# A fused transformer program on one core: token sums moved from GpSimd to VectorE, and a new order of VectorE's and ScalarE's work inside the feed-forward units

## The reference

```python
def swiglu(h, w1, w3, w2):
    return (jax.nn.silu(h @ w1) * (h @ w3)) @ w2      # w1, w3: 1024 x 2816, w2: 2816 x 1024

h = modulate(rms_norm(x), sh2, sc2)                   # layers 1 and 2
x = x + g2[:, None, :] * swiglu(h, ffn_w1[layer], ffn_w3[layer], ffn_w2[layer])
...
x = x + 0.5 * swiglu_2(rmsnorm(x, ffn1_norm[l]), ffn1_w_gu[l], ffn1_w_down[l])   # before and after the last mixer
```

## Time and profile before

| what | value |
|---|---|
| median of 3 executions | 2495.84 us (2491.64 to 2504.05) |
| the profiled execution: its own time | 2495.73 us |
| the profiled execution: span | 2493.9 us |
| mean granted clock of PE | 0.977 of full speed |
| PE busy | 2379.2 us, 95% |
| DVE busy | 1653.4 us, 66% |
| ACT busy | 999.2 us, 40% |
| POOL busy | 225.8 us, 9% |
| mean DMA rate | 130 GB/s |

### The profile page before, as it was taken

One profiled execution on the slowest core, in us unless ns is written; L12 is line 12 of the kernel. 1 busy time (PEld: TensorE's weight loads), 2 busy tenths in 40 slices (PEclk: granted clock), 3 DMA queues, 4 the chain that ended last, 5 costly groups with the idle time before them and its releaser, 6 DMA issues. The chain is left out here.

```text
span 2493.9 us, 35153 instructions
## 1 busy us (share of the span) xinstructions
PE 2379.2 (95%) x14848; PEld 2112.3 (85%) x14848; DVE 1653.4 (66%) x1985; ACT 999.2 (40%) x1369; POOL 225.8 (9%) x189
## 2 busy tenths in 40 slices
PE   7979999899999989999989999999999999999998
PEld 6658899888899869998869997879889877899986
DVE  6687689757755656884277885456678545688844
ACT  3453343323444443442243442244456544443322
POOL 0210301000013020000040000000000002300000
PEclk9998999999999999999989999999999999999999
DMA  8124577655233126663326653222212212466421
GB/s 347 65 84 186 164 225 205 194 208 196 70 125 104 57 70 175 179 155 119 102 86 166 188 137 123 89 95 85 85 46 74 85 68 85 123 180 170 131 100 68
DMA packets 71727, 325.04 MB, mean 130 GB/s; under 512 B 7850, under 2 KB 9130, under 8 KB 49810
## 3 DMA queue, kind: packets, MB, share of 16 engines
q1 hardware_dynamic: 51984, 238.75, 27.8%
q0 software_dynamic: 16208, 78.13, 13.1%
q10 hardware_dynamic: 3378, 5.91, 0.9%
HBM read 320.52 MB, written 2.24 MB: 129 GB/s over the span
## 5 line engine op out<-in xcount | busy, mean ns | idle before, releaser
L240 PE MATMUL bank<-h_hi,w_hi 128*128 128x256 f32 (+1 forms) x1512 | 512.9, 339 | 30.0 <-DVE w_lo L908 17.9
L241 PE MATMUL bank<-h_lo,w_hi 128*128 128x256 f32 (+1 forms) x1512 | 502.6, 332 | 0.0
L242 PE MATMUL bank<-h_hi,w_lo 128*128 128x256 f32 (+1 forms) x1512 | 502.5, 332 | 0.0
L227 DVE TENSOR_TENSOR w_lo<-raw,w_hi 128x2048 fp32r<-128x2048 f32 x120 | 279.4, 2329 | 145.2 <-ACT w_hi L223 145.2
L240 PEld LDWEIGHTS bank<-h_hi,w_hi 128*128 128x128 f32 x1512 | 291.9, 193 | 67.3 <-DVE w_lo L908 20.9
L242 PE MATMUL bank<-t_hi_tile,w_lo 128*128 128x256 f32 x1152 | 326.0, 283 | 0.0
L240 PE MATMUL bank<-t_hi_tile,w_hi 128*128 128x256 f32 x1152 | 326.0, 283 | 0.0
L241 PE MATMUL bank<-t_lo_tile,w_hi 128*128 128x256 f32 x1152 | 326.0, 283 | 0.0
L242 PEld LDWEIGHTS bank<-h_hi,w_lo 128*128 128x128 f32 x1512 | 291.5, 193 | 27.2
L241 PEld LDWEIGHTS bank<-h_lo,w_hi 128*128 128x128 f32 x1512 | 291.9, 193 | 26.0 <-issue 1.4
L240 PE MATMUL bank<-g_hi,w_hi 128*128 128x512 f32 x704 | 276.9, 393 | 17.6 <-DVE w_lo L227 9.0
(11 more groups left out here) (363 smaller groups left out, 4284.8 us busy)
## 6 DMA issues: line engine op xcount, KB each, us to landing
raw<-stream SPq DMA_DIRECT2D x120, 1024.0 KB, 4.9
raw<-stream SPq DMA_DIRECT2D x72, 512.0 KB, 4.5
work<-stream SPq DMA_DIRECT2D x72, 512.0 KB, 7.1
work<-stream POOLq DMA_DIRECT2D x72, 512.0 KB, 5.8
work<-stream POOLq DMA_DIRECT2D x19, 1024.0 KB, 7.2
raw<-stream SPq DMA_DIRECT2D x72, 256.0 KB, 5.9
h_plain<-stream POOLq DMA_DIRECT2D x16, 1024.0 KB, 5.3
work<-stream SPq DMA_DIRECT2D x13, 1024.0 KB, 12.3
```

What stands on the lines that cost most here:

```text
L227: nc.vector.tensor_tensor(w_lo[:, slot(m), :], raw[:, slot(m), :], w_hi[:, slot(m), :], ALU.subtract).then_inc(lo_split, 1)
L240: nc.tensor.matmul(out, stationary[0], moving[0], start=first, stop=False)
L241: nc.tensor.matmul(out, stationary[0], moving[1], start=False, stop=False)
L242: return nc.tensor.matmul(out, stationary[1], moving[0], start=False, stop=last)
```

## The change

It edits only the feed-forward stages, in six places.

1. The five token sums run on DVE (`hidden_sums`), behind the first unit's split in ffn0 and ffn1 and behind the second's in ffn2 and ffn3; there ACT writes the scaled tokens (`hidden_scaled`). POOL is left with DMAs alone. `hidden_high` and `hidden_low` follow accordingly, the low part one unit later than before.
2. In each fast unit `make_further` stands behind `mixes_low`, and `whole_low` directly behind `add_last`, ahead of `gate_chunk`. `make_further(0)` moves in the same way.
3. SP's loads of unit r wait for `make_further(r - 2)` ("s4") as well. The mixes of units 0 and 1 get a place of their own, and their load waits for the norm's last low part (`h_ready`) instead of `hidden_low`.
4. The conditioning additions stand at r = 1, 3, 5, 7, 9, 11, 14, the first ahead of the loop, and `write_mod` ahead of `add_last(16)`.
5. At the border, ACT makes `pair_high(0)` and the high part of `md` ahead of `keep_first(17)`.
6. PE's first down unit runs both halves over the four early banks before it turns to the last unit's four banks, and there waits for `add_last(17)` instead of `gate_chunk(17)`.

```diff
             def load(self, sp, m):
                 sp.wait_ge(lo_split, m - 1)
+                if r >= 2:
+                    sp.wait_ge(part_lo, self.part_low("s4", r - 2))
...
-                sp.wait_ge(part_lo, self.hidden_lows(2) if r < 2 else self.part_low("mixes", r - 2))
-                sp.dma_start(self.mixes[s], src[:, q:3 * q]).then_inc(landed[s], 16)
+                if r < 2:
+                    sp.wait_ge(h_ready, KC * self.norm.n + KC)
+                else:
+                    sp.wait_ge(part_lo, self.hidden_lows(3) if r < 4 else self.part_low("mixes", r - 2))
+                sp.dma_start(self.mixes(r), src[:, q:3 * q]).then_inc(landed[s], 16)
...
+            def hidden_scaled(self, act):
+                for k in range(KC):
+                    ins = nc.scalar.activation(self.norm.t[:, k, :], x[:, k, :], ACT.Copy, scale=self.norm.scale(k))
+                ins.then_inc(part_hi, 1)
+
+            def hidden_sums(self, dve, st):
+                if self.norm.deferred:
+                    dve.wait_ge(part_hi, self.hidden_highs(1))
...
+                    ins = nc.vector.tensor_tensor(out, one, two, ALU.subtract)
+                    if i < 4:
+                        st.link(ins)
+                ins.then_inc(part_lo, 1)
...
             def scalar(self, act, st):
                     if j < 2:
                         split_next_hi(act, m)
-                    if j == 0:
+                    if j == 0 and self.norm.deferred:
+                        self.hidden_scaled(act)
+                    if j == self.norm.deferred:
                         self.hidden_high(act)
...
                     if r + 1 < FAST:
                         self.whole_high(act, r + 1)
+                    else:
+                        self.pair_high(act, 0)
+                        act.wait_ge(products, self.product_done(4, r))
+                        split_hi(act, self.md)
                     self.keep_first(act, r)
                     if r + 1 < FAST:
                         self.mixes_high(act, r + 1)
-                self.pair_high(act, 0)
-                act.wait_ge(products, self.product_done(4, FAST - 1))
-                split_hi(act, self.md)
...
             def vector(self, dve, st):
                     if j < 2:
                         split_next_lo(dve, self.m0 + j)
-                    if j == 0:
+                    if j == self.norm.deferred:
+                        self.hidden_sums(dve, st)
+                    if j == 1 + self.norm.deferred:
                         self.hidden_low(dve)
                     if j == self.CONV - 2:
-                        self.make_further(dve, 0)
                         self.whole_low(dve, 0)
+                        if self.ada:
+                            dve.wait_ge(part_lo, self.hidden_lows(3))
+                            conditioning.add_unit(dve, 3 * KC)
                 self.mixes_low(dve, 0)
-                if self.ada:
-                    conditioning.add_unit(dve, 3 * KC)
+                self.make_further(dve, 0)
                 for r in range(FAST):
                     self.further_low(dve, r)
+                    if self.ada and r == FAST - 1:
+                        conditioning.write_mod(dve, st, 3)
                     if r:
                         self.add_last(dve, r - 1)
                     if r + 1 < FAST:
-                        self.make_further(dve, r + 1)
+                        self.whole_low(dve, r + 1)
                     if r:
                         self.gate_chunk(dve, r - 1)
                     if r + 1 < FAST:
-                        self.whole_low(dve, r + 1)
                         self.mixes_low(dve, r + 1)
+                        self.make_further(dve, r + 1)
...
                     self.add_first(dve, r)
-                    if self.ada and r and r % 2 == 0 and r < 16:
-                        conditioning.add_unit(dve, 3 * KC + r // 2)
+                    if self.ada and r in (1, 3, 5, 7, 9, 11, 14):
+                        conditioning.add_unit(dve, 3 * KC + 1 + (1, 3, 5, 7, 9, 11, 14).index(r))
...
                     if first:
-                        order = [(k, o) for k in range(2) for o in others + early + after]
+                        order = [(k, o) for k in range(2) for o in others + early] + [(k, o) for k in range(2) for o in after]
...
                         if first and k == 0 and o == after[0]:
-                            pe.wait_ge(gated, self.j0 + FB)
+                            pe.wait_ge(halves_added, self.added(4, late))
```

More of the change, by code:

```diff
@@ L783, in block, with mixes @@
                 return self.weights({"a12": 0, "a11": 1, "a22": 2, "s3": 4, "s1": 5, "s2": 6, "s4": 7}[n], 1)
+            def mixes(self, r):
+                return area((21504 if r < 2 else 4096) + UNIT // 2 * (r % 2), UNIT // 2)
             def mixes_in(self, r):
@@ L789, in part_done @@
             def part_done(self, name, r):
-                return self.hidden_highs(2) + 3 * r + {"mixes": 1, "further": 2, "first": 3}[name]
+                return self.hidden_highs(2 + self.norm.deferred) + 3 * r + {"mixes": 1, "further": 2, "first": 3}[name]
             def part_low(self, name, r):
-                return self.hidden_lows(2) + 4 * r + {"s2": 1, "s4": 2, "mixes": 3, "further": 4}[name]
+                return self.hidden_lows(3) + 4 * r + {"mixes": 1, "s2": 2, "s4": 3, "further": 4}[name]
             def product_done(self, n, r):
@@ L816, in add_parts @@
                 pool.wait_ge(landed[s], landings(self.fast(r)))
-                pool.dma_start(self.mixes[s], stream[place_of(self.fast(r)), :, 2 * q:], accum_op=ALU.add).then_inc(
+                pool.dma_start(self.mixes(r), stream[place_of(self.fast(r)), :, 2 * q:], accum_op=ALU.add).then_inc(
                     mixed_in[s], 16)
             def gpsimd(self, pool):
-                t = self.norm.t
-                if self.norm.deferred:
[L824 to L830, removed]
+                if self.ada:
+                    pool.wait_ge(ada_used, 24)
+                    pool.wait_ge(h_ready, KC * self.norm.n + KC)
+                    for n in range(24, 26):
+                        load_ada(pool, n)
+                for r in range(FAST):
+                    self.add_parts(pool, r)
+                    if self.ada and r in (2, 4, 6, 8, 10, 14):
+                        n = 26 + (2, 4, 6, 8, 10, 14).index(r)
+                        pool.wait_ge(ada_used, n if n == 31 else n - 1)
+                        load_ada(pool, n)
+            def hidden_scaled(self, act):
[3 more added lines that the diff above has]
+            def hidden_sums(self, dve, st):
+                if self.norm.deferred:
+                    dve.wait_ge(part_hi, self.hidden_highs(1))
+                v = self.norm.t.rearrange("p (a z) n -> p a z n", z=2)
                 n = self.HALF
@@ L917, in mixes_high @@
                     act.wait_ge(unit_used, self.fast(0))
-                nc.scalar.activation(self.weights(4, 2)[0], self.mixes[s], ACT.Copy).then_inc(part_hi, 1)
+                nc.scalar.activation(self.weights(4, 2)[0], self.mixes(r), ACT.Copy).then_inc(part_hi, 1)
             def mixes_low(self, dve, r):
@@ L1221, in tensor @@
                         self.norm.spread_row(pe)
[L1222 removed]
+                pe.wait_ge(part_lo, self.hidden_lows(3))
                 for r in range(FAST):
```

34 lines of the change are left out of this document (8 added, 26 removed).

## The result

| | before | after |
|---|---|---|
| median | 2494.67 us (2490.76 to 2504.05, 7 executions) | 2517.3 us (2510.84 to 2518.1, 7 executions) |
| ratio, 95% interval | | 1.0085 [1.0068, 1.0102] |
| span of the profiled execution | 2493.9 us | 2515.3 us |

The change makes the kernel slower by 22.6 us, 0.9%. The forecast was +7.9 us, in a range that ends at 2520.

What follows compares the result with a forecast made beforehand. PE, busy 95%, was taken to bound the kernel, with DVE's rounds exceeding its pace after the change. Fast units and border +27.9, down order -1.5, prologue -18.5 gave +7.9 us: 2504 us, 8 in 10 range 2488 to 2520.

Steps and rivals of the forecast that it cites:

- rival A: The forecast itself: fast-unit rounds of 10.40 and 11.12 us, own range 2494 to 2515 us; chance 0.64.
- B: Fast units: the transfer loop takes over at 11.4 us per unit, +24 us, 2528 us; chance 0.12.
- D: Prologue: sums on DVE only shift the wait, 10 us of the 18.5 are missing, 2514 us; chance 0.12.
- The round: Fast units: DVE's time per unit becomes 10.40 us, 11.12 where the norm is deferred, against PE's 10.08.
- the 1.93 us of the gate and the pair: Fast units: gate_chunk (0.60) and make_further's two instructions (1.33), free during DVE's wait for ACT before, now lengthen DVE's round.
- idle ahead of L919: Sign in fast units: DVE waits for ACT's whole_high some 2.1 us (2.8 deferred) in nearly every unit, 150 us in all.
- PE's waits for the low part of the whole unit: Sign in fast units: these waits grow from 17.9 to some 50 us, about 1 us each in ffn2 and ffn3.
- pair waits for no transfer in this sum: Fast units: the round's sum counts no transfer wait for make_further's two instructions.
- Rival C: Fast units: the waits simply go, rounds stay below 10.08 us, 2445 us in all; chance 0.12.
- The border: From the end of whole_low(17) to the first down product: load of md, high and low parts, 15.3 us.
- The new order of the first down unit: Border: 24 matmuls instead of 12 run ahead of the last unit's sums; taken as -1.5 us in all.
- The prologue: Ahead of the fast units, sums on DVE: -5.4, -5.4, -9.0 and +1.3 us for ffn0 to ffn3, sum -18.5.

Runs made afterwards that it cites:

- e1: The kernel after with DVE's old order back (make_further and gate_chunk ahead of whole_low) and without the loads' added wait: 2460.62 us, 0.988 of before.
- e4: The kernel before with only DVE's new order in the fast units and the loads' added wait: 2537.41 us, 1.0183 of before.
- e9: The kernel after with gate_chunk ahead of whole_low again, make_further staying behind mixes_low: 2493.29 us, 1.0001 of before.
- e10: The kernel after with make_further ahead of whole_low again, gate_chunk staying behind it: 2456.13 us, 0.9852 of before.
- e3: The kernel after with the mixes' accumulating DMA cut to 128 of 1024 columns, leaving out the other sums: 2510.72 us, one execution.
- e6: The kernel after with the old border: ACT's and PE's old order there, write_mod behind gate_chunk(17): 2520.7 us, 1.0115 of before.
- e5: The kernel after with the five token sums of each stage back on POOL: 2523.89 us, 1.0126 of before.

## Why the prediction was right, and where it was short

The mechanism was right, its size was not: the loss is nearly three times the +7.9 us that were said. The measured 2517.3 lies 2.3 us beyond the range of the forecast itself, rival A's 2494 to 2515. It lies within the stated 2488 to 2520 only because that leaves room for B and D. D did not happen, and of B only single late transfers; that it held the result was luck. The chances stood at 0.47 for no change and 0.40 for slower by over 0.5%; it is slower by 0.85%.

**The round (10.40 and 11.12 us).** Measured 10.41 and 11.13, with an addition 12.67 (10.40 + 2.26). That the 1.93 us of the gate and the pair were free before and cost in full after is shown by e1 (late units recur at 8.47 us again), by e4 (10.40 and 11.13), and in two doses by e9 and e10. Most stated signs are there: idle ahead of L919 of 2.07 us in every steady round (2.1 was said; the 2.8 of the deferred stages did not come), 133.8 in all (150 was said). One is not: PE's waits for the low part of the whole unit were to grow from 17.9 to some 50 us; they are 13.8, and 21.4 stand at L987, which the list had not named.

**Rival A against B: the term that was short.** The step "the pair waits for no transfer in this sum" is true, and L947 waits for none. But ACT's `mixes_high` does, 17.6 us in 9 waits, of which these are four:

```profile
960.71 1.06 ACT L929 ACTIVATE w_hi<-work 128x1024 fp32r<-128x1024 f32 x1 [1.71 <-DMA work<-stream]
983.16 1.06 ACT L929 ACTIVATE w_hi<-work 128x1024 fp32r<-128x1024 f32 x1 [2.58 <-DMA work<-stream]
1329.36 1.06 ACT L929 ACTIVATE w_hi<-work 128x1024 fp32r<-128x1024 f32 x1 [2.08 <-DMA work<-stream]
2197.14 1.06 ACT L929 ACTIVATE w_hi<-work 128x1024 fp32r<-128x1024 f32 x1 [2.98 <-DMA work<-stream]
```

I asked for B whether the transfer loop is longer than the round on average (17.7 us for two units: no) and gave single late landings no price. But where DVE's round is above PE's there is no slack to take them up. What adds is not ACT's whole wait but the part in which DVE stands still ahead of L934: 1.0 to 2.3 us in seven of the nine units, 10.3 in all, and nothing in the other two, where ACT waited 0.66 and 0.92 us. By so much, and the overlap of two instructions that goes with it, these seven rounds are longer than 10.41, 12.67 or 11.13 us. In the sum it is 4.7 + 4.4 + 1.4 + 2.3 = 12.8 us at the 17th low part; e3 takes the late transfers away and 11.0 of them go. Of the other 1.8 us, 1.2 lie in ffn0: there `whole_high(17)` waits for PE, which had the sums of the conditioning (L343) to make in between. Rival C counted PE's time for them (1.9 us), the forecast did not:

```profile
477.41 1.49 ACT L913 ACTIVATE w_hi<-raw 128x1536 fp32r<-128x1536 f32 x1 [1.00 <-PE bank L242]
```

Before, a round of 8.47 us caught up 1.6 us in each unit. The late transfers, taken at nothing in the sum, are the step that failed, by size and not by sign.

**The border (15.3 us).** Measured 15.9, 15.6, 15.8, 15.8: 1.9 us short in all. The new order of the first down unit I had priced at -1.5; e6 finds nothing.

**The prologue (-18.5, with the -1.5 above -20.0).** Measured -21.1 outside the stages. The prologues proper, from the first product of a stage to its first fast product, took 50.4, 51.3, 59.3 and 45.4 us before and take 45.1, 45.2, 51.2 and 46.7 now: -5.3, -6.2, -8.1 and +1.3, in all -18.3 (-5.4, -5.4, -9.0 and +1.3 were said). The other -2.8 lie where of the edits only the new order of the first down unit acts, -2.6 of them between the first down product of ffn0 and the start of ffn1. That stretch took 399.5 to 405.2 us in the twelve kernels; why it varies was not tried. Five linked sums took 6.25 (6.3). The reason given, additions slowed by POOL's work beside them, is shown for ffn2: 13.52 to 5.46 us, and e5, where POOL makes the sums but not beside L454, keeps 5.46. The 3.7 us of ACT for the high parts and the wait of 1.17 ahead of the first fast product (1.3 said) are there as well.

**The Trainium skill.** Its advice (Perfetto Trace Analysis, Optimizing Scalar/DVE Operations) to give work of a saturated DVE to GpSimd was weighed against the window of the prologue. The row held: DVE is not saturated there, and with the sums on it the four prologues are 6.2 us shorter than in e5. The prediction left out what the same section goes on to say, that GpSimd and DVE share an SBUF read port, so that moving work between these two might not help; the rows of e5 agree with that (below).

**Together:** 7.9 + 12.8 + 1.9 - 1.1 = 21.5 us, the difference of the spans. Rival C (the waits simply go) falls with the rounds above 10.08; with shorter rounds e10 comes to 2456, against C's 2445. Rival D falls with the prologue.

## What to carry to other kernels

A wait for a transfer can be taken away by moving its reader later in the list, but what the reader stood in front of matters as much: ahead of `whole_low` it filled a gap that another engine's chain sets, behind it, it lengthens the round. So write the round of each engine as a sum, with its gaps, and look which instructions fill a gap; only then move them. And once another engine's round is above that of PE, give each single late transfer a price, and not only the average: it is the time for which that engine itself stands still, here 10.3 of the 17.6 us that ACT waited.

## What the runs showed of the hardware that was not expected

**DVE beside POOL.** In e5 a DVE subtraction of 128 x 4 takes 2.36 us beside POOL's sums, and 0.16 in the kernel after, where POOL is idle:

```profile
908.21 0.16 DVE L880 TENSOR_TENSOR small<-mod 128x4 f32<-128x4 f32 x1
```

The split behind it takes 3.88 in place of 2.29. POOL is slowed too. Its twenty sums (shortest, median and longest in ns), and the first one in ffn1:

```profile
L837 POOL TENSOR_TENSOR work<-work x20: 2385/2394/4396, 250.9 to 2169.3; 128x1024 f32<-128x1024 f32 x20
910.31 4.38 POOL L837 TENSOR_TENSOR work<-work 128x1024 f32<-128x1024 f32 x1 [95.89 <-DVE h_lo L480]
```

The split that DVE began at 910.15 ends at 912.43, and POOL's sum ends 2.26 us later, at 914.69. The small instruction ends at 914.72. So it does not run slower in proportion: it waits for one sum of POOL to end, as that sum had waited for the split. L1113, a multiplication with one input in SBUF and one in PSUM, takes 0.69 us beside POOL's second sum, as L1099 does in the kernel after. The Trainium skill (SBUF — State Buffer, Who interferes with whom) says that a DVE instruction with two SBUF inputs contends with a GpSimd instruction that reads SBUF, that one with a single SBUF input does not, and that the one that issued first keeps the shared ports for its whole instruction while the other blocks. These rows agree, and so does L454 with 13.52 against 5.46 us for seven.

**The clock at the border.** Ahead of the first down product PE now waits longer. The ten microseconds from that product on (us, busy time and instructions of PE, PEld, DVE, ACT, POOL, then the granted clock, DMA share, GB/s), in ffn2 and ffn3 of the kernel after:

```profile
1512.58:1522.58 10.00, 10.00 (x35) 8.07 (x36) 8.26 (x9) 3.38 (x3) 0.00 (x0) 0.79 0.36 112
2380.36:2390.36 10.00, 10.00 (x37) 8.16 (x38) 8.26 (x9) 3.39 (x3) 0.00 (x0) 0.83 0.33 107
```

and of before:

```profile
1503.84:1513.84 10.00, 8.35 (x35) 6.58 (x36) 8.26 (x9) 3.38 (x3) 0.00 (x0) 1.00 0.34 108
2358.52:2368.52 10.00, 9.91 (x35) 7.71 (x36) 8.26 (x9) 3.39 (x3) 0.00 (x0) 0.83 0.32 106
```

A mean of 0.79 or 0.83 is a mix of the two levels, 1.2 and 2.4 GHz. After a wait of 4.65 us the clock falls for a part of these windows; after before's wait of 3.14 us it stays at 1.00 in ffn2 and falls in ffn3 (0.83), so the length of the wait does not settle it. The longer wait costs nothing by the clock: from the first down product to the start of the last of the stage's 528 matmuls it is 122.0, 121.0, 121.6 and 121.6 us before and 121.0, 122.1, 121.5 and 121.1 after. In e1, where PE waits 1.90 to 2.44 us ahead of the same product in ffn1 to ffn3, the clock stays at 1.00 there and these stretches take 119.6 us each.
